# One of eight later modulation vectors computed on TensorE beside layer 1's input projection instead of on VectorE beside layer 0's FFN

## The chip, the cores and the metric

The kernel runs on one core of one Trainium2 chip. The metric is device time in microseconds (us), the median of several executions.

## The reference

Two layers of a backbone are applied to 128 context tokens and 128 latent tokens of width 2048. Both streams go through the same weights, each with its own modulation. Cut to what matters, one layer is:

```
m = silu(cond) @ w_mod + b_mod                 # 2048 x 12288, cut in six vectors of 2048
sm, cm, gm, sf, cf, gf = split(m, 6)           # vectors 0 to 5 of the layer
h = rms_norm(x, g_pre) * (1 + cm) + sm
z = h @ w_in                                   # 2048 x 4608
o = attention A, attention B, gated mixing of z
x = x + gm * rms_norm(o @ w_out, g_post)       # 2048 x 2048
h = rms_norm(x, g) * (1 + cf) + sf
x = x + gf * rms_norm((silu(h @ w_gate) * (h @ w_up)) @ w_down, g2)   # inner width 5632
```

`cond` is `c_ctx` for the context and `c` for the latent tokens. With two layers there are twelve modulation vectors. Each needs a 2048 x 2048 block of `mod_w` (16.8 MB in f32) for two rows of output. Vector 8 is layer 1's `gm`, the gate of its mixer: it is first needed when layer 1's attention begins.

## The kernel before

All weights are streamed from HBM once, in pieces of 256 rows by 512 columns (512 KB). A dense product runs in units of eight pieces (one chunk of 512 output columns). For each piece SyncE issues the load into `raw` (a ring of four slots), ScalarE casts it to `whi` (line 1094), VectorE makes the remainder `wlo` (line 1362), and TensorE does 12 matmuls of 512 columns (line 792): two halves of the piece, two token streams, three products (`whi,xt_lo`, `wlo,xt_hi`, `whi,xt_hi`). The rings have four slots (`RING`) and ScalarE and VectorE split four pieces ahead of TensorE (`LEAD`). All pieces have one running number g. Layer 0's FFN is g 104 to 367, layer 1's input projection ("win 1" below) g 368 to 439, layer 1's output projection g 440 to 471, layer 1's FFN g 472 to 735. An FFN is cut in three groups: up and gate units, then the down units of the group. Layer 0's down groups start at g 168, 264 and 344. The last one has four chunks of six pieces (g 344 to 367).

The modulation vectors are computed beside this, in either of two ways.

On TensorE (`MOD_PE`, `mod_quarter`, line 852): a vector is 32 pieces of `mod_w`, put in the ring `mraw` (four slots), as four chunks of eight. A burst of four pieces is 8 matmuls, each recorded as two rows; they put 32 columns of `cond` against 512 columns of weights, and four of them go to four separate partition groups of bank M. After the last chunk, ScalarE copies bank M to `mrow` (line 1123), TensorE turns it (`vector_turn`, line 872) and VectorE copies bank T to `modt` (line 1403). Before, vectors 2 (beside layer 0's input projection), 3 and 4 (attention and output projection of layer 0), 9 and 10 (the same of layer 1) go this way; layer 1's input projection carries none.

On VectorE (`MOD_DVE`): at certain g, right behind the split of piece g, `accumulate` multiplies one 128 x 1024 piece of `mod_w` by one element of `cond` per partition and adds it to `acc`, once for each of the two conditions (line 1384, or 1381 for the first of a sum). When the 32 pieces of a vector are in, TensorE sums over the partitions (line 782, `MOD_REDUCE`, behind its piece g), ScalarE copies the row behind its cast of piece g + 3 (`MOD_ROW`), TensorE turns it behind piece g + 2 (`MOD_TAIL`), VectorE copies it behind its split of g + 9 (`MOD_COLS`). Before, vectors 5, 6, 7 and 8 go this way in layer 0's FFN, 128 pieces spread evenly over g 111 to 363, and vector 11 in layer 1's FFN.

Work of an engine runs in the order of the program. On VectorE, where an up group ends, the order is: the splits of the unit (which reach four pieces into the down group), `multiply` (line 1750, makes `hid`), later `ht_lo` (line 1757). TensorE, behind the first piece of the down group, waits for `hid` to transpose it (line 880). In the last down group VectorE also adds each chunk to `f` (line 1793) and multiplies by the gate (line 1587); ScalarE squares `f` between (line 1108).

SyncE issues all weight loads in one order. A `raw` load waits until the slot's piece was split (`lo_ready`), a `mod_w` load waits in `mod_room` until the piece four earlier in the ring `mraw` was used; whatever is behind it in the program waits with it.

Between two stages lies a turnover: `rms_norm` of the finished rows, the new x, its transposes. Its last part overlaps the first four pieces of the next stage, which TensorE takes for one token stream, then for the other (`APART`).

Of the kernel before, what the change touches and what calls it, by code (L numbers as in the profile page):

```python
# [17 lines left out]
CH = 512  # L18
# [5 lines left out]
W_INC = W_IN // CH  # L24
# [13 lines left out]
UNIT = KD // KB  # L38
RING = 4
LEAD = 4  # L40
# [3 lines left out]
IN_FIRST, IN_SECOND = {3: range(0, 4)}, {3: range(4, 8)}  # L44
LOAD_ONE = {0: [0], 1: [1], 2: [2], 3: [3], 4: [4], 5: [5], 6: [6], 7: [7]}
LOAD_FIRST, LOAD_SECOND = ({0: [j], 2: [j + 1], 4: [j + 2], 6: [j + 3]} for j in (0, 4))
# [3 lines left out]
MOD_WIN = W_INC // 2  # L50
# [3 lines left out]
APART = 4  # L54
# [17 lines left out]
def edge_of(l, which):  # L72
# [4 lines left out]
OUT_MODS = {3: (0, range(0, 4)), 8: (0, range(4, 8)), 13: (1, range(0, 4)), 19: (1, range(4, 8)), 24: (2, range(0, 4))}  # L77
OUT_FETCH = {4: (0, (0, 1)), 5: (0, (2, 3)), 11: (0, (4, 5)), 12: (0, (6, 7)), 16: (1, (0, 1)), 17: (1, (2, 3)),
             22: (1, (4, 5)), 23: (1, (6, 7)), 27: (2, (0, 1)), 28: (2, (2, 3)), 31: (2, (4, 5, 6, 7))}
MOD_PE = [2, 3, 4, 9, 10]  # L80
MOD_DVE = [5, 6, 7, 8, 11]
MPIECES = 2 * KD
FFN_PIECE = [104, 472]
DVE_SPAN = 252


def dve_piece_at(v, i):

    if v == 11:
        return FFN_PIECE[1] + 8 + 5 * i // 2  # L90
    return FFN_PIECE[0] + 7 + DVE_SPAN * (MPIECES * MOD_DVE.index(v) + i) // (4 * MPIECES - 1)


def dve_reduce_at(v):

    return dve_piece_at(v, MPIECES - 1)
# [3 lines left out]
MOD_FETCH = {g - 3: e for g, e in DVE_PIECES.items()}  # L100
MOD_REDUCE = {dve_reduce_at(v): v for v in MOD_DVE}
MOD_TAIL = {dve_reduce_at(v) + 2: v for v in MOD_DVE}
MOD_ROW = {dve_reduce_at(v) + 3: v for v in MOD_DVE}
MOD_COLS = {dve_reduce_at(v) + 9: v for v in MOD_DVE}


def dve_op(v, i, s=0):
# [80 lines left out]
class Plan:  # L188
# [3 lines left out]
    def __init__(self):  # L192
        self.unit, self.mod, self.use = 0, 0, dict.fromkeys(BANKS, 0)

        self.fills, self.fill = dict.fromkeys(BANKS, 0), {}
        self.at = {}
        self.turn_bank = 0
        self.acc_bank = 0

        self.mark(("init",))  # L200
        self.take("X0")
        self.mods(MOD_INIT)
        for l in range(DEPTH):
            self.pre(l, 0)
            self.mark((l, "win"))
            self.unit += W_INC
            self.mods(0 if l else MOD_WIN)
            self.takes(["A0", "A1"], (W_INC + 1) // 2 if l else ND * W_INC // 2)
            self.takes(["B0", "B1"], W_INC // 2 if l else ND * W_INC // 2)
            self.mark((l, "att"))  # L210
            self.attention(l)
            self.mark((l, "out"))
            self.unit += ND
            self.takes(["A0", "A1", "B0", "B1"], ND // 2)
            self.mods(MOD_OUT + 1)
            self.pre(l, 1)
            for g, (_, n) in enumerate(GROUPS):
                self.mark((l, "up", g))
                self.unit += 2 * n
                self.takes(["A0", "A1", "B0", "B1", "X0", "X1"], n)  # L220
                if g == 1:
                    self.gate(l, 1)
                self.mark((l, "down", g))
                self.unit += n if n < 4 else ND
                self.takes(["A0", "A1", "B0", "B1"], ND // 2)
# [56 lines left out]
def build_program(nc, a):  # L282
    plan = Plan()
# [7 lines left out]
    with ExitStack() as ctx:  # L291
# [192 lines left out]
        def _(sp):  # L484
# [44 lines left out]
            def both(u, w, col, m=0, l=0, behind={}, js=range(UNIT)):  # L529

                for j in js:
                    piece(u, j, w[j * KB * P:(j + 1) * KB * P, bass.ds(col, CH)])
                    if j in behind:
                        mod_chunk(m, l, behind[j])
# [29 lines left out]
                    mod_chunk(m, 0, js)  # L564
            for l in range(DEPTH):
                if l:
                    u, _, _ = plan.at[(l, "win")]
                    w = a["w_in"][l]
                    both(u, w, 0, js=range(LEAD, UNIT))
                    for i in range(1, W_INC):  # L570
                        both(i + u, w, i * CH)
                u, m, _ = plan.at[(l, "out")]
                w = a["w_out"][l]
                first_unit(u, w, 0)
                for step, _, m_att in plan.at[(l, "attention")]:
                    if step[0] == "mod_first":
                        mod_chunk(m_att, l)
                for q in range(LEAD, ND * UNIT):
                    i, j = divmod(q, UNIT)
                    both(u + i, w, i * CH, js=[j])  # L580
                    if q in OUT_FETCH:
                        mi, js = OUT_FETCH[q]
                        mod_chunk(m + mi, l, js)
                first_unit(plan.at[(l, "up", 0)][0], a["w_gate"][l], 0)
                for g, (c0, n) in enumerate(GROUPS):
                    u, _, _ = plan.at[(l, "up", g)]
                    both(u, a["w_gate"][l], c0 * CH, js=range(0 if g else LEAD, UNIT))
                    for i in range(0, n - 1):
                        chunk(i * 2 + (u + 1), a["w_up"][l], 0, i * CH + c0 * CH)
                        chunk(i * 2 + (u + 2), a["w_gate"][l], 0, i * CH + (c0 + 1) * CH)  # L590
                    chunk(u + 2 * n - 1, a["w_up"][l], 0, (c0 + n - 1) * CH)
                    u, m, _ = plan.at[(l, "down", g)]
                    if n == 4:
                        for i in range(0, ND):
                            chunk(i + u, a["w_down"][l], c0 * CH, i * CH)
                    else:
                        for i in range(ND):
                            chunk(u, a["w_down"][l], c0 * CH, i * CH, 2 * n, 2 * n * i)
                if l + 1 < DEPTH:
                    first_unit(plan.at[(l + 1, "win")][0], a["w_in"][l + 1], 0)  # L600
# [137 lines left out]
        def _(pe):  # L738
# [8 lines left out]
            def dense(u, pair, i, hi, lo, nk=KD, ph=0, ready=None, m=None, behind={}, first=0, last=0):  # L747

                free(pair + "0", i)
                free(pair + "1", i)
                n = nk // KB
                for js in (range(first), range(first, n - last), range(n - last, n)):
                    together = js.start == first and js.stop == n - last
                    for streams in [(0, 1)] if together else [(0,), (1,)]:
                        for j in js:
                            if streams[0] == 0:
                                pe.wait_ge(lo_ready, u * UNIT + (ph + j + 1))
                            slot = (ph + j) % RING  # L760
                            for kb in range(KB):
                                k = j * KB + kb
                                if ready:
                                    ready(k, streams)
                                mm = products(pair, k, hi, lo, slot, kb, nk, streams=streams)
                            if streams[-1] == 0:
                                if j == n - 1:
                                    mm.then_inc(half_done, 1)
                                continue
                            mm.then_inc(w_used, 1)  # L770
                            if j in behind:
                                mod(m, behind[j])
                            dve_vector(u * UNIT + ph + j)
# [222 lines left out]
            pe.wait_ge(cond_ready, 1)  # L996
            start()
            for l in range(DEPTH):
                u, _, use = plan.at[(l, "win")]

                def pair(i, ready=None):
                    dense(i * 2 + u, "A", i + use["A0"], xt_hi, xt_lo, ready=ready, first=APART if ready else 0)
                    dense(i * 2 + (u + 1), "B", i + use["B0"], xt_hi, xt_lo)

                if l:
                    pair(0, pre(l, 0))
# [59 lines left out]
        def ahead(split, u, ph=0, pieces=UNIT, between=None, leave=0, late=None):  # L1066


            for j in range(pieces - leave):
                split(u, ph + LEAD + j)  # L1070
                if late:
                    late(j)
                if between and j == pieces - 1 - max(leave, 1):
                    between()
# [8 lines left out]
        def _(act):  # L1083
# [190 lines left out]
                    square(x[:, s, n * CH:(n + 1) * CH], ssx[:, s, n:n + 1])  # L1274
            start()
            for l in range(DEPTH):
                u, _, _ = plan.at[(l, "win")]
                if l:
                    ahead(split, u, late=lambda j: pre_late(l, 0, j))
                    for i in range(1, W_INC):  # L1280
                        ahead(split, i + u)
                attention(l)
                u, m, use = plan.at[(l, "out")]
                for i in range(ND):
# [60 lines left out]
        def _(dve):  # L1345
# [363 lines left out]
            normal(0, 0, 0, 1, 2, 3)  # L1709
            start()  # L1710
            for l in range(DEPTH):
                u, _, use = plan.at[(l, "win")]

                def pair(i):
                    ahead(split, i * 2 + u, late=None if i else lambda j: pre_late(l, 0, j))
                    read_out(i * 2 + u, i * 2 * CH, "A")
                    ahead(split, i * 2 + (u + 1))
                    read_out(i * 2 + (u + 1), i * 2 * CH + CH, "B")

                if l:  # L1720
                    for i in range(W_INC // 2):
# [119 lines left out]
```

## Time and profile before

| | us |
|---|---|
| median of 3 runs | 2442.37 |
| lowest, highest | 2436.07, 2445.17 |
| the profiled execution, its own time | 2445.17 |
| its span (first to last instruction) | 2443.4 |
| TensorE busy / VectorE busy / ScalarE busy | 2310.0 / 1578.3 / 984.4 |

The profile is one execution. Its span is 1.8 us less than its time. Shares of busy time are averages over stages; what an edit is worth is read in the stage where it acts. The three runs lie 9.1 us apart.

### The profile page before, as it was taken

The numbers are of one execution on the slowest core, as the hardware profiler recorded it, in microseconds if no ns is written. First come the engines' busy times: TensorE is split into PE (matmuls) and PEld (weight loads), VectorE is DVE, ScalarE is ACT, GpSimd is POOL, SyncE is SP. The second block draws the span as 40 slices with busy tenths as digits, with TensorE's granted clock in tenths as the row PEclk, the third lists the DMA queues.
The fourth block names the chain that finished last, engine by engine and source line by source line (L and its number), as shares of the span: only waits on it lengthen the run. The fifth ranks groups of instructions, "written<-read, shape, count | busy, mean of one in ns | idle before, by whom it ended". The sixth has DMA issues, their size and how long they took to land.

```text
span 2443.4 us, 28114 instructions
## 1 busy us (share of the span) xinstructions
PE 2310.0 (95%) x10780; PEld 1806.2 (74%) x10780; DVE 1578.3 (65%) x1715; ACT 984.4 (40%) x1253; POOL 67.5 (3%) x97
## 2 busy tenths in 40 slices
PE   4999878989999999999998998798999999999998
PEld 1776645768878888788776885576888888878886
DVE  2555444479988889889886454446888644554455
ACT  2333232454444444334345344335444444434443
POOL 1000020000000000000000102000000000000000
PEclk8999988999999999999999999999999999999999
DMA  8779978858878878788864766885877666656664
GB/s 302 254 281 340 332 274 288 303 193 303 284 254 299 288 265 293 246 280 289 298 198 155 215 208 233 286 300 197 278 268 252 220 196 189 189 182 192 191 221 147
DMA packets 269319, 609.93 MB, mean 250 GB/s; under 512 B 19117, under 2 KB 19297, under 8 KB 267841
## 3 DMA queue, kind: packets, MB, share of 16 engines
q1 hardware_dynamic: 264832, 589.37, 71.5%
q0 software_dynamic: 4352, 18.76, 2.2%
q8 instruction: 86, 1.41, 0.2%
q14 instruction: 49, 0.39, 0.0%
HBM read 603.79 MB, written 5.45 MB: 249 GB/s over the span
## 4 chain that ended last, share of the span: by engine, by line
PE 84%; DMA 6%; DVE 4%; issue 2%; ACT 2%; SPq 0%; POOL 0%; DVEq 0%; POOLq 0%; ACTq 0%
PE bank_A L792 39%; PE bank_B L792 38%; DMA mraw<-in_mod_w 6%; PE bank_M L852 3%; PE bank_X L880 2%; DVE wlo L1362 1%; PE bank_M L841 1%; ACT whi L1094 1%; PE bank_T L872 1%; DVE xtmp L1443 1%; DVE x L1475 0%; DMA raw<-in_w_out 0%; DVE acc L1384 0%; PE bank_M L782 0%; ACT xtmp L1137 0%
## 5 line engine op out<-in xcount | busy, mean ns | idle before, releaser
L1362 DVE TENSOR_TENSOR wlo<-raw,whi 128x1024 fp32r<-128x1024 f32 x736 | 896.7, 1223 | 687.2 <-ACT whi L1094 687.0
L1094 ACT CAST whi<-raw 128x1024 fp32r<-128x1024 f32 x736 | 770.3, 1050 | 1190.8 <-PE bank_A L792 591.3
L792 PE MATMUL bank_A<-whi,xt_lo 128*128 128x512 f32 x1136 | 452.1, 398 | 17.9 <-DVE xt_lo L1413 11.1
L792 PE MATMUL bank_A<-wlo,xt_hi 128*128 128x512 f32 x1136 | 446.8, 393 | 0.0
L792 PE MATMUL bank_A<-whi,xt_hi 128*128 128x512 f32 x1136 | 446.5, 393 | 0.0
L792 PE MATMUL bank_B<-whi,xt_lo 128*128 128x512 f32 x1104 | 433.4, 393 | 0.5 <-issue 0.5
L792 PE MATMUL bank_B<-wlo,xt_hi 128*128 128x512 f32 x1104 | 430.0, 389 | 0.0
L792 PE MATMUL bank_B<-whi,xt_hi 128*128 128x512 f32 x1104 | 429.7, 389 | 0.0
L1384 DVE SCALAR_TENSOR_TENSOR acc<-mraw,cond,acc 128x1024 f32<-128x1024 f32 x300 | 371.2, 1279 | 0.0
L792 PEld LDWEIGHTS bank_A<-whi,xt_lo 128*128 128x128 f32 x1136 | 215.9, 190 | 84.5 <-issue 28.1
L792 PEld LDWEIGHTS bank_A<-whi,xt_hi 128*128 128x128 f32 x1136 | 215.8, 190 | 46.0
L792 PEld LDWEIGHTS bank_B<-whi,xt_lo 128*128 128x128 f32 x1104 | 207.3, 188 | 56.2 <-issue 13.4
L792 PEld LDWEIGHTS bank_A<-wlo,xt_hi 128*128 128x128 f32 x1136 | 215.9, 190 | 43.5
L792 PEld LDWEIGHTS bank_B<-whi,xt_hi 128*128 128x128 f32 x1104 | 207.2, 188 | 43.6
L792 PEld LDWEIGHTS bank_B<-wlo,xt_hi 128*128 128x128 f32 x1104 | 207.3, 188 | 42.0
L792 PE MATMUL bank_A<-whi,ht_lo 128*128 128x512 f32 x352 | 139.2, 395 | 0.7 <-DVE wlo L1362 0.7
L792 PE MATMUL bank_A<-wlo,ht_hi 128*128 128x512 f32 x352 | 138.3, 393 | 0.0
L792 PE MATMUL bank_A<-whi,ht_hi 128*128 128x512 f32 x352 | 137.9, 392 | 0.0
L792 PE MATMUL bank_B<-whi,ht_lo 128*128 128x512 f32 x352 | 137.5, 391 | 0.2 <-DVE wlo L1362 0.2
L792 PE MATMUL bank_B<-wlo,ht_hi 128*128 128x512 f32 x352 | 137.0, 389 | 0.0
L792 PE MATMUL bank_B<-whi,ht_hi 128*128 128x512 f32 x352 | 137.0, 389 | 0.0
L852 PE MATMUL bank_M<-mraw,cond 128*32 128x512 f32 x640 | 93.4, 689 | 30.7 <-DMA mraw<-in_mod_w 30.7
(193 smaller groups left out, 1432.9 us busy)
## 6 DMA issues: line engine op xcount, KB each, us to landing
mraw<-in_mod_w SPq DMA_DIRECT2D x384, 512.0 KB, 6.0
raw<-in_w_gate SPq DMA_DIRECT2D x176, 512.0 KB, 4.4
raw<-in_w_up SPq DMA_DIRECT2D x176, 512.0 KB, 4.4
raw<-in_w_down SPq DMA_DIRECT2D x176, 512.0 KB, 4.8
raw<-in_w_in SPq DMA_DIRECT2D x144, 512.0 KB, 4.7
raw<-in_w_out SPq DMA_DIRECT2D x64, 512.0 KB, 5.8
gate_mix<-gate_rows POOLq DMA_DIRECT2D x4, 1024.0 KB, 6.6
gate_ffn<-gate_rows POOLq DMA_DIRECT2D x4, 1024.0 KB, 9.0
```

Of the source, the lines that this page charges most:

```text
L792: mm = pe.matmul(bank[f"{pair}{s}"][:], xs[:, k, t], ws_[:, slot, kb, :], start=(k == first and n == 0), stop=(k == (nk - 1 if last is Non ...
L841: mm = pe.matmul(bank["M"][g:g + 32, :], cond[:, 2 * k:2 * k + 32], mraw[:, j % RING, kb, :], start=(k < 4), stop=(k >= KD - 4))
L852: mm = pe.matmul(bank["M"][32 * c:32 * c + 32, :], cond[:, 2 * k:2 * k + 32], mraw[:, ring_piece(m, j + c // 2) % RING, c % 2, :], start=( ...
L872: mm = pe.matmul(bank["T"][:, w * t:w * t + w], mrow[:, t * P:(t + 1) * P], sel[:], start=True, stop=True)
L880: mm = pe.transpose(bank[b][:, n * P:(n + 1) * P], t, ident[:])
L1094: act.copy(whi[:, ph % RING], raw[:, ph % RING]).then_inc(hi_ready, 1)
L1362: dve.tensor_tensor(wlo[:, ph % RING], raw[:, ph % RING], whi[:, ph % RING].bitcast(F32), ALU.subtract).then_inc(lo_ready, 1)
L1384: ins = dve.scalar_tensor_tensor(out=acc[:, h, s, :], in0=w, scalar=c, in1=acc[:, h, s, :], op0=ALU.mult, op1=ALU.add)
L1443: ins = dve.tensor_scalar(xtmp[:, b % 2, s, t, :], bank[bk][:, t * P:(t + 1) * P], scal[:, k, s:s + 1], shift[:, k, s:s + 1], ALU.mult, AL ...
```

## The change

Vector 8 moves from `MOD_DVE` to `MOD_PE`. The planner gives layer 1's input projection four chunks of modulation, like layer 0's: a burst of four pieces behind the fourth piece of each of its first eight units, the row and turn behind the eighth unit. The loads of these 32 pieces are put between the `raw` loads of those units (`LOAD_FIRST`, `LOAD_SECOND`: behind the loads of pieces 0, 2, 4, 6 of a unit; the first two ahead of the unit's fifth piece). `IN_FIRST`, `IN_SECOND`, `LOAD_FIRST` and `LOAD_SECOND` were in the file already. Vectors 5, 6 and 7 keep VectorE and are now placed at g = 112, 196, 280 plus 5i/2 rounded down, for i from 0 to 31 (so five splits carry two pieces). Each ends 77 pieces after its start, at g 189, 273 and 357. The row copy on ScalarE moves from g + 3 to g + 5 behind the reduction, the column copy on VectorE from g + 9 to g + 8; this holds for vector 11 too.

```
-MOD_PE = [2, 3, 4, 9, 10]
-MOD_DVE = [5, 6, 7, 8, 11]
+MOD_PE = [2, 3, 4, 8, 9, 10]
+MOD_DVE = [5, 6, 7, 11]
-DVE_SPAN = 252
+DVE_FIRST = {5: FFN_PIECE[0] + 8, 6: FFN_PIECE[0] + 92, 7: FFN_PIECE[0] + 176, 11: FFN_PIECE[1] + 8}
 def dve_piece_at(v, i):
-    if v == 11:
-        return FFN_PIECE[1] + 8 + 5 * i // 2
-    return FFN_PIECE[0] + 7 + DVE_SPAN * (MPIECES * MOD_DVE.index(v) + i) // (4 * MPIECES - 1)
+    return DVE_FIRST[v] + 5 * i // 2
-MOD_ROW = {dve_reduce_at(v) + 3: v for v in MOD_DVE}
-MOD_COLS = {dve_reduce_at(v) + 9: v for v in MOD_DVE}
+MOD_ROW = {dve_reduce_at(v) + 5: v for v in MOD_DVE}
+MOD_COLS = {dve_reduce_at(v) + 8: v for v in MOD_DVE}
...
-            self.mods(0 if l else MOD_WIN)
+            self.mods(MOD_WIN)
...
-                    u, _, _ = plan.at[(l, "win")]
+                    u, m, _ = plan.at[(l, "win")]
                     w = a["w_in"][l]
-                    both(u, w, 0, js=range(LEAD, UNIT))
-                    for i in range(1, W_INC):
-                        both(i + u, w, i * CH)
+                    both_rest(u, w, 0, m, l)
+                    both(u + 1, w, CH, m, l, LOAD_SECOND)
+                    for i in range(1, W_INC // 2):
+                        both(i * 2 + u, w, i * 2 * CH, i + m, l, LOAD_FIRST)
+                        both(i * 2 + (u + 1), w, i * 2 * CH + CH, i + m, l, LOAD_SECOND)
+                    both(u + W_INC - 1, w, (W_INC - 1) * CH)
...
-                    dense(i * 2 + u, "A", i + use["A0"], xt_hi, xt_lo, ready=ready, first=APART if ready else 0)
-                    dense(i * 2 + (u + 1), "B", i + use["B0"], xt_hi, xt_lo)
+                    dense(i * 2 + u, "A", i + use["A0"], xt_hi, xt_lo, ready=ready, m=i + m, behind=IN_FIRST,
+                          first=APART if ready else 0)
+                    dense(i * 2 + (u + 1), "B", i + use["B0"], xt_hi, xt_lo, m=i + m, behind=IN_SECOND)
+                    mod_tail(i + m)
...
-                    for i in range(1, W_INC):
-                        ahead(split, i + u)
+                    ahead(split, u + 1, between=lambda: mod_row(m))
+                    for i in range(1, W_INC // 2):
+                        ahead(split, i * 2 + u)
+                        ahead(split, i * 2 + (u + 1), between=lambda: mod_row(i + m))
+                    ahead(split, u + W_INC - 1)
...
                     read_out(i * 2 + (u + 1), i * 2 * CH + CH, "B")
+                    mod_cols(i + m)
```

## Rows read from the trace of the kernel before

**Rows 1.** The page: busy time of the engines, and the chain that ended last

```profile
PE 2310.0 (95%) x10780; PEld 1806.2 (74%) x10780; DVE 1578.3 (65%) x1715; ACT 984.4 (40%) x1253; POOL 67.5 (3%) x97
PE 84%; DMA 6%; DVE 4%; issue 2%; ACT 2%; SPq 0%; POOL 0%; DVEq 0%; POOLq 0%; ACTq 0%
```

**Rows 2.** Busy us by stretch (PE, PEld, DVE, ACT, POOL), PE clock, DMA share, GB/s

```profile
549.25:1206.65 657.40, 651.93 (x2940) 535.47 (x2939) 576.28 (x523) 271.57 (x286) 0.55 (x1) 1.00 0.82 280
1206.65:1282.10 75.45, 71.78 (x320) 56.60 (x319) 61.42 (x67) 31.97 (x46) 1.64 (x3) 0.98 0.68 233
1282.10:1315.40 33.30, 24.48 (x104) 18.80 (x104) 26.73 (x53) 21.10 (x44) 2.02 (x3) 0.85 0.31 95
1315.40:1500.00 184.60, 182.85 (x816) 149.85 (x816) 96.19 (x89) 70.95 (x69) 9.22 (x13) 1.00 0.70 216
1720.00:2366.60 646.60, 644.33 (x2891) 532.08 (x2890) 385.56 (x347) 269.76 (x284) 0.55 (x1) 1.00 0.67 214
```

**Rows 3.** Chain of work: start us, us; a unit in layer 0's FFN, one in win 1

```profile
571.01 21.77 PE bank_A L792 x96
...
1342.90 21.76 PE bank_A L792 x96
```

**Rows 4.** Timeline of TensorE, a burst in layer 1's output projection: start us, us

```profile
1593.29 1.92 PE L852 MATMUL bank_M<-mraw,cond 128*32 128x512 f32 x16
1595.14 0.50 PE L792 MATMUL bank_A<-whi,xt_lo 128*128 128x512 f32 x1
```

**Rows 5.** Timeline of TensorE: vector 8's reduction and turn, with the matmul behind each

```profile
1267.56 1.92 PE L782 MATMUL bank_M<-acc,ones_row 128*32 128x512 f32 x16
...
1269.41 0.50 PE L792 MATMUL bank_B<-whi,ht_lo 128*128 128x512 f32 x1
...
1278.28 0.95 PE L872 MATMUL bank_T<-rsel,mrow 128*128 128x8 f32 x8
1279.09 0.48 PE L792 MATMUL bank_B<-whi,ht_lo 128*128 128x512 f32 x1
```

**Rows 6.** Timeline of VectorE and TensorE at the starts of four down groups

```profile
706.62 0.39 PE L792 MATMUL bank_A<-whi,ht_hi 128*128 128x512 f32 x1
708.20 0.99 PE L880 MATMUL bank_X<-ident,hid 128*128 128x128 f32 x6 [1.19 <-DVE wlo L1362]
...
978.99 2.48 DVE L1384 SCALAR_TENSOR_TENSOR acc<-mraw,cond,acc 128x1024 f32<-128x1024 f32 x2
...
979.00 0.39 PE L792 MATMUL bank_A<-whi,ht_hi 128*128 128x512 f32 x1
982.16 1.21 PE L880 MATMUL bank_X<-ident,hid 128*128 128x128 f32 x8 [2.78 <-issue]
...
1213.54 0.63 PE L792 MATMUL bank_A<-wlo,ht_hi 128*128 128x512 f32 x1
1213.97 0.63 PE L792 MATMUL bank_A<-whi,ht_hi 128*128 128x512 f32 x1
...
1877.32 0.39 PE L792 MATMUL bank_A<-whi,ht_hi 128*128 128x512 f32 x1
1878.08 1.10 PE L880 MATMUL bank_X<-ident,hid 128*128 128x128 f32 x7 [0.38 <-issue]
```

**Rows 7.** Timeline of TensorE from layer 0's last down group into the turnover

```profile
1256.45 0.50 PE L792 MATMUL bank_A<-whi,ht_lo 128*128 128x512 f32 x1 [0.67 <-DVE wlo L1362]
...
1272.65 0.50 PE L792 MATMUL bank_B<-whi,ht_lo 128*128 128x512 f32 x1 [0.19 <-DVE wlo L1362]
1285.76 1.97 PE L880 MATMUL bank_X<-ident,f 128*128 128x128 f32 x8 [3.70 <-DVE f L1429]
```

**Rows 8.** Raw loads of win 1, then of 1388 to 1392, issue to landing

```profile
DMA to landing us min/median/max: 4.2/4.5/11.8
...
DMA to landing us min/median/max: 8.9/10.3/11.8
```

**Rows 9.** Timeline of ScalarE in win 1 while GpSimd's attention loads run

```profile
1403.40 1.05 ACT L1094 CAST whi<-raw 128x1024 fp32r<-128x1024 f32 x1 [4.60 <-DMA raw<-in_w_in]
```

More of the change, by code:

```diff
@@ L998, in _ @@
             for l in range(DEPTH):
-                u, _, use = plan.at[(l, "win")]
+                u, m, use = plan.at[(l, "win")]
                 def pair(i, ready=None):
-                    dense(i * 2 + u, "A", i + use["A0"], xt_hi, xt_lo, ready=ready, first=APART if ready else 0)
-                    dense(i * 2 + (u + 1), "B", i + use["B0"], xt_hi, xt_lo)
+                    dense(i * 2 + u, "A", i + use["A0"], xt_hi, xt_lo, ready=ready, m=i + m, behind=IN_FIRST,
+                          first=APART if ready else 0)
+                    dense(i * 2 + (u + 1), "B", i + use["B0"], xt_hi, xt_lo, m=i + m, behind=IN_SECOND)
+                    mod_tail(i + m)
                 if l:
@@ L1276, in _ @@
             for l in range(DEPTH):
-                u, _, _ = plan.at[(l, "win")]
+                u, m, _ = plan.at[(l, "win")]
                 if l:
                     ahead(split, u, late=lambda j: pre_late(l, 0, j))
-                    for i in range(1, W_INC):
-                        ahead(split, i + u)
+                    ahead(split, u + 1, between=lambda: mod_row(m))
[3 more added lines that the diff above has]
+                    ahead(split, u + W_INC - 1)
                 attention(l)
@@ L1711, in _ @@
             for l in range(DEPTH):
-                u, _, use = plan.at[(l, "win")]
+                u, m, use = plan.at[(l, "win")]
                 def pair(i):
```

## The prediction

> **What bounds the kernel now.** I read the page first: TensorE is busy 95% of the span, and 84% of the chain that ended last is TensorE's own work, against 4% of VectorE [rows 1]. So I looked at where TensorE is not the bound. The busy time by stretch compares the two FFNs, which do the same dense work [rows 2]. Layer 0's runs with VectorE busy 576.28 of 657.40 us (88%), layer 1's with 385.56 of 646.60 (60%), and TensorE is busy over 99% in both. The chain shows a unit of 96 matmuls at 21.77 us in layer 0's FFN and 21.76 in win 1 [rows 3], that is 0.227 us a matmul and 2.72 a piece. A saturated VectorE beside it does not slow a unit. What VectorE costs layer 0's FFN must lie in gaps between units. I went through TensorE's timeline for these, from the start of one matmul to the start of the next, in both FFNs.
>
> **What the change adds.** Vector 8 needs 32 pieces, in eight bursts. In the timeline of layer 1's output projection a burst starts at 1593.29 and the next dense matmul at 1595.14 [rows 4]: 1.85 us in which TensorE does nothing else. The ten full bursts of the two output projections that stand between dense matmuls all read so. Win 1 is 182.85 us busy of 184.60 [rows 2], so no idle time takes them in. Eight bursts: 8 x 1.85 = +14.8. The first comes in the turnover, behind piece g 371, ahead of the last transpose of x; the casts and subtractions that follow that transpose end just when TensorE wants piece 374, so it counts in full too. The turn of the row, 0.81 (1278.28 to 1279.09, [rows 5]), is now paid behind the eighth unit: +0.8. ScalarE's row copy stands one piece (2.72) ahead of it, more than its cast and copy take; the copy of bank T on VectorE is covered by the unit after. Together +15.6 in win 1.
>
> **What it removes on TensorE.** Vector 8's reduction, from 1267.56 to the matmul at 1269.41, is 1.85, and its turn 0.81 [rows 5]: -2.7. So TensorE's own work grows by 12.9.
>
> **What VectorE's relief gives.** 32 pieces of two accumulations (2.48 us a pair, [rows 6]) leave VectorE in layer 0's FFN, some 79 us. Most of that is idle time handed to an engine that was not the bound. It counts only at the gaps I found:
>
> 1. Where a down group starts, TensorE waits after one piece for `hid`. Without an accumulation near it the gap is 0.76 (1877.32 to 1878.08, layer 1, [rows 6]). An accumulation behind the last split ahead of `multiply` stands in front of it: 979.00 to 982.16, 3.16, with the pair on VectorE at 978.99 [rows 6]. One behind the split before that, as at 706.62 to 708.20, makes it 1.58 [rows 6]. The old formula for the places gives pieces at g 168 and 170, at 265 and 267, and at 345 and 347; the last split ahead of `multiply` is g 171, 267, 347. The traced gaps fit that. The new places are 169; 266; 345 and 347. So the first group goes from 1.58 to 0.76 (-0.8), the second from 3.16 to 1.58 (-1.6), the third stays at 3.16.
> 2. Behind the long gaps matmuls run at 0.43 a step (1213.54 to 1213.97, [rows 6]) instead of 0.227 for a few us: seven or eight of them, 1.5 us. That goes in the second group with its gap (-1.5) and stays in the third.
> 3. In the last down group old pieces stand every other g up to 363, ten of them; of the new ones six, the last at 357. TensorE waits for `wlo` at 1256.45 (0.67) and 1272.65 (0.19) [rows 7], with the slower steps around them 1.1 in all; layer 1's group, with no accumulations, has next to none. With two pieces instead of three in the second chunk, and none behind it, I reckon VectorE ready some 2 us before it is wanted: -1.1.
>
> Sum: -0.8 - 1.6 - 1.5 - 1.1 = -5.0. The later row copy costs nothing: at g + 5 ScalarE waits for g + 1, and cast and copy end inside piece g + 2. Vector 7's reduction and turn now lie in the third chunk of the last down group, ahead of the turnover, at their old price. The turnover itself loses the row copy on ScalarE and the small copy on VectorE, off the chain I followed; I count nothing, and keep as a bound TensorE's wait of 3.70 at its start [rows 7].
>
> **The queue of SyncE.** Each `mod_w` load of a unit waits for the burst of the unit before. Behind it stands `raw` piece 1 of the next unit, which would have gone out when piece 5 was split, about 3.8 us earlier. I worked out its slack in TensorE pieces: issued just after the burst of a unit begins, it is wanted 15.4 us after that begins, less 2.3 for cast and subtraction; it lands in 4.5 us, the median of win 1 [rows 8]. That leaves about 8, so no stall. Traffic in win 1 goes from 216 GB/s [rows 2] to 284 (216 over 184.6 us is 39.9 MB; with 16.8 MB more in 200 us), which layer 0's FFN holds (280, [rows 2]) with no stall.
>
> **Total.** +15.6 - 2.7 - 5.0 = +7.9 us, say +8. Against the profiled execution's own 2445.17 that is 2453; that execution was the slowest of three, 2.8 above the median, so for the median of the new kernel I take 2442.4 + 8 = 2450.4.
>
> Bounds: if none of the three gains comes, +12.9; if all that sets layer 0's FFN apart from layer 1's goes (the third long gap with its slow steps, 4.0 more), +4. The best end adds the turnover's wait of 3.70: +0.
>
> **Rivals.**
>
> *SyncE's order starves TensorE in win 1 (slower).* For it: one queue carries both rings, and a blocked `mod_w` load holds the `raw` loads. The weak place is where GpSimd's attention loads run: `raw` landings rise to a median of 10.3 and at most 11.8 us [rows 8], and a ScalarE cast starts after 4.60 us of waiting [rows 9]; TensorE did not wait. Its slack there is about 14.3 us from issue to landing. If extra traffic and the 3.8 us of blocking add 5 us to the worst landing, TensorE loses 2 to 3 us once: +11. If it happens at every unit, at 3 us each, +8 + 8 x 3 = +32, or 2474. It decides from the point where landings pass 12 to 13 us regularly. Against it: layer 0's FFN runs one `mod_w` load to two `raw` loads all through, the same mix, and the blocking thins traffic just then.
> The Trainium skill (DMA: Bandwidth & Descriptors, Queues, rings and completion order) says that a DMA engine with work in several queue rows alternates between them. By that rule SyncE's queue has half of the engines while GpSimd's loads run; over 12 us (the longest landing) at half of 280 GB/s that is 3.2 pieces, where 4.4 `raw` pieces and half as many of `mod_w` are wanted: 3.4 pieces short, or 6.4 us at full rate, against about 10 of slack (14.3 less the median landing). The trace's late cast agrees with the rule for the old traffic; for the new it would put the case at the edge, which is why I give the rival more than a token chance.
>
> *VectorE's relief gives nothing (slower by 13).* The gaps are set by ScalarE or loads, not by accumulations. Against it: the three groups' gaps follow the places of the accumulations exactly. 2455.3.
>
> *The turnover gains (faster).* With no accumulation in its last two chunks, the turnover behind layer 0's FFN could lose its idle time and its low clock: 33.30 us at a clock of 0.85, 24.48 busy [rows 2]. Even all of the 8.8 idle us leaves -1, no measurable gain; faster by over 0.5% would also need bursts that hide, and [rows 4] speaks against that.
>
> **How the numbers follow.** About 0.5% (12 us) is what a measurement of this kernel can tell from no change. My sum stands at +0.3%. Its own range is +4 to +13, with 4 us of scatter between medians (three runs spread over 9.1 us). Chances: the sum 0.72 (0.60 within 0.5%, 0.10 slower, 0.02 faster through scatter); starving 0.13 (0.11 slower); no relief 0.10 (0.06 slower); turnover gain 0.05 (0.02 faster). That makes faster 0.04, same 0.69, slower 0.27. The range: low 2441 (the best bound less a little scatter), high 2463 (no relief, a few us of starving, scatter).
>
> **What would show it.** Rows of line 852 in win 1, x16 and eight of them, each 1.85 to the next dense matmul; the stage 15 to 16 us longer with TensorE still 99% busy; no TensorE wait on `raw` or `wlo` in it. The gaps at the starts of layer 0's down groups: 0.76, 1.58, 3.16. VectorE busy some 79 us less in layer 0's FFN and the stretch from its start to the turnover 7 to 8 us shorter. It would be wrong if TensorE waits for `wlo` or for `mraw` in win 1, if bursts there cost other than 1.85, if new waits arise at vector 7's reduction in the last down group, or if the turnover changes by more than 2 us.

## The result, and the profile after

| | before | after |
|---|---|---|
| median of 11 runs each, us | 2445.17 | 2457.20 |
| lowest to highest | 2436.07 to 2449.35 | 2446.18 to 2463.11 |
| ratio of after to before | | 1.0053, 95% interval 1.0038 to 1.0068 |
| profiled execution, its own time | 2445.17 | 2467.93 |
| its span | 2443.4 | 2466.1 |

The change makes the kernel slower by 0.53%, 13 us by the ratio (9 to 17) and 12.0 by the medians. I had said +8, with +4 to +13 for the likeliest case alone. My 2450.4 stood on the median of three runs, 2442.37; with eleven runs the kernel before is at 2445.17, so 2.8 of the 6.8 us between 2450.4 and 2457.20 lie in the base and 4.0 in the sum. The profiled execution of after happens to be slower than all eleven timed ones, 10.7 us over their median; its stages are therefore read beside a second profile of each kernel below.

The page of the changed kernel, its busy times by engine (share of the span, instructions):

```profile
PE 2332.2 (95%) x10892; PEld 1816.3 (74%) x10892; DVE 1507.0 (61%) x1651; ACT 984.2 (40%) x1253; POOL 67.5 (3%) x97
```

VectorE is 71.3 us less busy than in [rows 1], where I had said some 79, and TensorE 22.2 more. The same stretches as in [rows 2], by their landmarks in the new trace (columns as there):

```profile
549.72:1203.14 653.42, 650.34 (x2916) 535.33 (x2915) 516.02 (x466) 270.61 (x285) 0.55 (x1) 0.99 0.79 260
1203.14:1277.06 73.92, 71.01 (x320) 56.80 (x319) 51.88 (x60) 31.42 (x44) 1.64 (x3) 0.98 0.69 225
1277.06:1314.61 37.55, 27.61 (x121) 20.50 (x122) 27.83 (x53) 22.41 (x47) 1.84 (x3) 0.82 0.42 127
1314.61:1514.70 200.09, 198.41 (x937) 152.79 (x935) 95.61 (x90) 71.08 (x69) 9.24 (x13) 1.00 0.79 270
1741.30:2389.30 648.00, 645.74 (x2891) 532.90 (x2890) 384.94 (x347) 269.70 (x284) 0.55 (x1) 1.00 0.69 213
```

Layer 0's FFN body is 4.0 us shorter with 60 us less on VectorE. Win 1 (fourth row) is 15.5 longer; TensorE fills 99% of it, and DMA moves 270 GB/s instead of 216. The trace has no wait of TensorE in win 1, and SyncE waits there for a burst six times, at most 6.4 us, at no cost to anyone.

A burst in win 1, in TensorE's timeline (start us, us):

```profile
1330.34 0.39 PE L793 MATMUL bank_B<-wlo,xt_hi 128*128 128x512 f32 x1
1330.57 0.39 PE L793 MATMUL bank_B<-whi,xt_hi 128*128 128x512 f32 x1
1330.89 1.92 PE L853 MATMUL bank_M<-mraw,cond 128*32 128x512 f32 x16
1332.74 0.50 PE L793 MATMUL bank_B<-whi,xt_lo 128*128 128x512 f32 x1
1333.08 0.40 PE L793 MATMUL bank_B<-wlo,xt_hi 128*128 128x512 f32 x1
```

From the burst to the next dense matmul it is 1.85 us, as in [rows 4]. But look at its neighbours: the step (from one start to the next) into the burst is 0.32 and the step behind it 0.34, where dense matmuls step by 0.227. The edges of a burst cost about 0.2 us more, which I had left out.

Then the starts of the three down groups of layer 0's FFN, to be read against [rows 6]:

```profile
707.25 0.39 PE L793 MATMUL bank_A<-whi,ht_hi 128*128 128x512 f32 x1
708.02 0.63 PE L881 MATMUL bank_X<-ident,hid 128*128 128x128 f32 x4 [0.38 <-issue]
...
975.72 0.39 PE L793 MATMUL bank_A<-whi,ht_hi 128*128 128x512 f32 x1
977.29 0.88 PE L881 MATMUL bank_X<-ident,hid 128*128 128x128 f32 x5 [1.19 <-DVE wlo L1368]
...
1205.47 0.39 PE L793 MATMUL bank_A<-whi,ht_hi 128*128 128x512 f32 x1
1208.63 1.94 PE L881 MATMUL bank_X<-ident,hid 128*128 128x128 f32 x8 [2.77 <-issue]
```

The gaps are 0.77, 1.57 and 3.16 us, where I had said 0.76, 1.58 and 3.16. Not as I had said: the matmuls behind the second group's start still run slow in this profile.

```profile
980.01 0.61 PE L909 MATMUL bank_X<-ident,gatev 128*32 128x128 f32 x2 [1.51 <-DVE ht_lo L1764]
980.55 0.79 PE L793 MATMUL bank_A<-whi,ht_lo 128*128 128x512 f32 x1
981.14 0.63 PE L793 MATMUL bank_A<-wlo,ht_hi 128*128 128x512 f32 x1
981.56 0.63 PE L793 MATMUL bank_A<-whi,ht_hi 128*128 128x512 f32 x1
```

The step is 0.42 (981.14 to 981.56) instead of 0.227; the granted clock from 981.0 to 984.5 is 0.50, that is the level of 1.2 instead of 2.4 GHz. So a gap of 3.16 us is not needed for slow steps. A second wait, of 1.51 us for `ht_lo` (1.49 in one profile), stands behind the gap in every version, and eleven slow steps follow it here. In the second profile of the same kernel, below, none follows it, and eight stand behind the third group's gap, where the first profile has one. Which of the two places runs slow is scatter in these profiles; what decides it is not shown. The wait at the turnover behind this FFN grew as well, from 3.70 [rows 7] to 4.45:

```profile
1276.66 0.39 PE L793 MATMUL bank_B<-whi,ht_hi 128*128 128x512 f32 x1
1281.50 0.90 PE L881 MATMUL bank_X<-ident,f 128*128 128x128 f32 x3 [4.45 <-DVE f L1435]
```

The turn of vector 8's row used to lie between the two token streams of the last chunk. VectorE's chain from the first stream's addition to `f` (1275.76 in before, 1271.65 in after) to this transpose takes 10.0 and 9.85 us in the two, so TensorE had time for the turn. Without it, most of its 0.81 us comes back here as waiting.

### The profile page after: what moved, and what is told of

It reads as the page before. It is cut to its first block, busy times and chain, and to the rows that moved or that the text cites. A ratio compares the mean times of both kernels' runs of the same rounds, so it can differ in the third digit from the quotient of the medians.

```text
span 2466.1 us, 28259 instructions
## 1 busy us (share of the span) xinstructions
PE 2332.2 (95%) x10892; PEld 1816.3 (74%) x10892; DVE 1507.0 (61%) x1651; ACT 984.2 (40%) x1253; POOL 67.5 (3%) x97
## 4 chain that ended last, share of the span: by engine, by line
PE 87%; DMA 5%; DVE 4%; ACT 2%; issue 1%; POOL 0%; SPq 0%; DVEq 0%; POOLq 0%; ACTq 0%
PE bank_A L793 40%; PE bank_B L793 38%; DMA mraw<-in_mod_w 5%; PE bank_M L853 3%; PE bank_X L881 2%; PE bank_M L842 1%; DVE wlo L1368 1%; DVE x L1481 0%; PE bank_T L873 0%; ACT whi L1097 0%; DVE xtmp L1449 0%; PE bank_M L783 0%; PE bank_B L970 0%; ACT junk L1111 0%; PE bank_A L970 0%
## 5 line engine op out<-in xcount | busy, mean ns | idle before, releaser
L1390 DVE SCALAR_TENSOR_TENSOR acc<-mraw,cond,acc 128x1024 f32<-128x1024 f32 x240 | 297.1, 1280 | 0.0
L793 PEld LDWEIGHTS bank_B<-whi,xt_lo 128*128 128x128 f32 x1104 | 207.2, 188 | 59.7 <-issue 16.8
L853 PE MATMUL bank_M<-mraw,cond 128*32 128x512 f32 x768 | 106.4, 662 | 32.1 <-DMA mraw<-in_mod_w 32.0
```

The source lines that it names most:

```text
L793: mm = pe.matmul(bank[f"{pair}{s}"][:], xs[:, k, t], ws_[:, slot, kb, :], start=(k == first and n == 0), stop=(k == (nk - 1 if last is Non ...
L853: mm = pe.matmul(bank["M"][32 * c:32 * c + 32, :], cond[:, 2 * k:2 * k + 32], mraw[:, ring_piece(m, j + c // 2) % RING, c % 2, :], start=( ...
L1390: ins = dve.scalar_tensor_tensor(out=acc[:, h, s, :], in0=w, scalar=c, in1=acc[:, h, s, :], op0=ALU.mult, op1=ALU.add)
```

## The experiments

Stretches below are read from TensorE's timeline in each profile: layer 0's FFN from the last transpose of x ahead of it (537.4 in before) to the first behind it (1285.8 in [rows 7]); the turnover from there to its last transpose of x (1309.3); win 1 from there to its last dense matmul (1494.8). "Slow" counts single dense steps of 0.36 to 0.45 us in layer 0's FFN.

The last column is the sum of the three stages against the mean of the two profiles of before.

| kernel | ratio to before (95%) | layer 0's FFN | slow | turnover | win 1 | sum |
|---|---|---|---|---|---|---|
| before | 1 | 748.4 | 14 | 23.5 | 185.6 | -0.4 |
| before, again | one time | 749.1 | 14 | 23.5 | 185.6 | +0.4 |
| after | 1.0053 (1.0038 to 1.0068) | 743.5 | 13 | 27.0 | 201.0 | +13.7 |
| after, again | one time | 741.1 | 9 | 25.4 | 201.0 | +9.7 |
| thin bursts | 0.9985 (0.9965 to 1.0004) | 741.1 | 7 | 23.8 | 189.6 | -3.3 |
| no vector 8 | 0.9956 (0.9942 to 0.9971) | 743.6 | 14 | 25.0 | 185.5 | -3.6 |
| after, free splits | 1.0023 (1.0006 to 1.0041) | 736.4 | 2 | 27.0 | 201.0 | +6.6 |
| after, all three hit | 1.0071 (1.0050 to 1.0092) | 750.3 | 23 | 27.0 | 201.0 | +20.5 |
| after, old row places | 1.0052 (1.0032 to 1.0071) | 741.0 | 8 | 25.4 | 201.0 | +9.7 |
| vector 8 on VectorE in win 1 | 0.9953 (0.9937 to 0.9970) | 737.9 | 7 | 23.3 | 187.7 | -8.9 |
| the same, after's places | 0.9969 (0.9956 to 0.9983) | 743.6 | 14 | 25.1 | 187.7 | -1.5 |
| before, three pieces moved by one | 0.9954 (0.9936 to 0.9972) | 741.8 | 6 | 23.6 | 185.6 | -6.9 |

**The kernel before again, and after again.** No edit.

> The kernel before once more, for a second profile. The two profiles so far differ by 7.0 us in the stretch from layer 1's attention to the end of its turnover, where the change edits nothing. If that is scatter of the waits on mod_w loads in the attention (one theory), this profile lies between or beyond the two (204 to 213 us from the last dense matmul of win 1 to the last transpose of x, known so far as 212.6 and 219.6). If the change causes it (the other), this profile repeats 212.6 within 1 us.

> The changed kernel once more. Scatter: its stretch from layer 1's attention to the last transpose of x is nearer to 212.6 than to 219.6 us. Caused by the change: 219 to 220 again. In both cases the ledger of the earlier stages repeats: layer 0's FFN 4 to 5 us shorter than before, win 1 15 us longer, and the turnover between them 3.5 us longer (1.85 of it the first burst).

Single times 2451.36 and 2453.67. The stretch in question, by its summed stages, is 220.0 us in the second profile of before (213.2 in the first; the expectation's figures start one row later) and 220.0 in the second of after: it is scatter. My expectation for after's second profile was wrong (it lay at the upper value, not the lower), but before reaches that value by itself. The scatter is not in the waits for `mod_w` loads, where I had looked for it. From the last dense matmul of win 1 to the first transpose of x, in the first and the second profile of before (columns as in [rows 2]):

```profile
1494.83:1684.33 189.50, 162.57 (x917) 110.85 (x915) 90.61 (x134) 75.31 (x143) 16.20 (x18) 0.95 0.78 275
```

```profile
1494.36:1689.08 194.72, 167.42 (x916) 113.58 (x915) 90.72 (x134) 75.28 (x143) 16.17 (x18) 0.92 0.77 267
```

TensorE waits 12.5 us for `mod_w` loads in the one and 12.0 in the other. What differs is its busy time, 4.9 us more for as many matmuls, at a granted clock of 0.92 instead of 0.95. The rest is the turnover behind, which takes 23.7 to 23.9 or 25.3 us, whatever the kernel. Over all twelve profiles this stretch takes 210.1 to 220.1 us (first part at a clock of 0.98 to 0.91), and the stretch ahead of layer 0's FFN, where no edit changes the work but for one `memset`, 529.1 to 538.0. The time of one profiled execution therefore says little about a few us. The sum of the three stages leaves this scatter out.

In the second profile of after the FFN is 7.6 us shorter than the mean of before's two and the turnover 1.9 longer, where I had expected 4 to 5 and 3.5; win 1 is 15.5 longer, and the sum is +9.7. The first profile gives -5.3, +3.5 and +15.5, +13.7 in all. Their mean is +11.7.

Its chain over win 1 shows the burst's full price (start us, us):

```profile
1307.25 10.88 PE bank_B L793 x48
1318.13 1.85 PE bank_M L853 x16
1319.98 11.15 PE bank_B L793 x48
1331.13 10.88 PE bank_A L793 x48
1342.01 1.85 PE bank_M L853 x16
1343.86 11.15 PE bank_A L793 x48
```

48 dense matmuls take 10.88 us ahead of a burst and 11.15 behind it: a burst costs 1.85 + 0.27 = 2.12. A unit with one is 23.88 us (1318.13 to 1342.01), one without 21.76 [rows 3]. The trace of before has the same price in layer 1's output projection, behind the burst of [rows 4], by its chain of work:

```profile
1593.36 1.85 PE bank_M L852 x16
1595.21 11.15 PE bank_A L792 x48
```

**Thin bursts.** Vector 8's matmuls stream 32 of their 512 columns. What is left out: 15 of 16 parts of vector 8. Loads and waits all stay.

```
             def mod_quarter(m, js):
+                n = 32 if vector_of(m) == 8 else CH
...
-                        mm = pe.matmul(bank["M"][32 * c:32 * c + 32, :], cond[:, 2 * k:2 * k + 32],
-                                       mraw[:, ring_piece(m, j + c // 2) % RING, c % 2, :], ...)
+                        mm = pe.matmul(bank["M"][32 * c:32 * c + 32, 0:n], cond[:, 2 * k:2 * k + 32],
+                                       mraw[:, ring_piece(m, j + c // 2) % RING, c % 2, 0:n], ...)
```

> The changed kernel, but vector 8's matmuls in win 1 stream 32 of the 512 weight columns (the rest of vector 8 is left out); all loads and waits stay. If TensorE's time in the bursts is what win 1 costs, a burst falls from 1.85 to 0.5 to 0.9 us and the kernel is 8 to 11 us faster than the changed one, about +2 to +4 over before. If the loads or SyncE's blocked order cost it, it stays at the changed kernel's +12.

Measured 0.9985: 16.6 us less than after by the two ratios, whose intervals are each some 4 us wide to either side; by the profile 11.4 in win 1 and 1.6 to 3.2 in the turnover. It is below the range I gave (2 to 4 us over before): layer 0's FFN is 7.6 us shorter in this profile, where the first profile of after had shown 4.9, and a thin burst is shorter than I thought:

```profile
1322.64 0.39 PE L793 MATMUL bank_B<-whi,xt_hi 128*128 128x512 f32 x1
1322.96 0.33 PE L855 MATMUL bank_M<-mraw,cond 128*32 128x32 f32 x16
1323.22 0.50 PE L793 MATMUL bank_B<-whi,xt_lo 128*128 128x512 f32 x1
1323.56 0.39 PE L793 MATMUL bank_B<-wlo,xt_hi 128*128 128x512 f32 x1
```

0.26 us a burst, with the same edges (0.32 into it, 0.34 behind it). All 16.8 MB are still loaded in the same order and TensorE waits for none of them: win 1 is 4.0 us longer than before, which is seven of these bursts with their edges (7 x 0.48 = 3.4) and the turn of 0.8. SyncE still waits for bursts here, up to 5.8 us, and the stage is within 0.2 us of what bursts and turn add up to. So loads and blocking cost nothing in win 1; the columns streamed on TensorE do.

**No vector 8.** Vectors 5 to 7 as in after; vector 8 is neither loaded nor computed, its columns are set to zero.

```
-MOD_DVE = [5, 6, 7, 8, 11]
+MOD_DVE = [5, 6, 7, 11]
+MOD_ALL = [2, 3, 4, 5, 6, 7, 9, 10, 11]
...
+            dve.memset(modt[:, 8 * KD * 2:9 * KD * 2], 0.0)
```

> Vectors 5, 6, 7 placed as in the changed kernel, vector 8 not computed anywhere and its 16.8 MB not loaded (its result is left out, set to zero). Against before this is VectorE's relief alone: by the prediction -5.0 -2.7 = -7.7 us; by the changed kernel's profile, where layer 0's FFN was only 4.9 shorter, -3 to -5. If relief gives nothing, -2.7. Against the thin-burst kernel it shows what loads and leftover bursts cost: 4 to 8 us if only the leftover bursts and the turn do, over 10 if the loads do.

`MOD_ALL` is the order in the ring and of the turns.

Measured 0.9956, 10.8 us less than before (7 to 14), more than either of my figures. The stages show 5.1 less in the FFN, 1.5 more in the turnover and nothing in win 1, -3.6 in all. In this kernel's and after's profiles the FFN is 5 to 8 us shorter; about 2 of that is vector 8's reduction, which TensorE no longer makes there, and 3 to 5.5 are relief. Had relief given nothing, -2.7 would have been measured, and the interval excludes that. What lies above the stages in the 10.8 I can assign to none; the profiled execution was the slowest of nine (2446.98 against a median of 2437.64). Between this kernel and the thin bursts lie 7.1 us by the two ratios, within my 4 to 8 for leftover bursts and the turn alone.

**Free splits.** One line of after; no accumulation behind g 170, 171, 266, 267, 346 or 347.

```
-DVE_FIRST = {5: FFN_PIECE[0] + 8, 6: FFN_PIECE[0] + 92, 7: FFN_PIECE[0] + 176, 11: FFN_PIECE[1] + 8}
+DVE_FIRST = {5: FFN_PIECE[0] + 8, 6: FFN_PIECE[0] + 89, 7: FFN_PIECE[0] + 174, 11: FFN_PIECE[1] + 8}
```

> The changed kernel with vector 6 placed from g 193 and vector 7 from g 278, so that no accumulation stands behind the last two splits ahead of a multiply (g 170, 171, 266, 267, 346, 347 all free). If accumulations there make the gaps at the starts of down groups, all three gaps are 0.76 to 0.77 us, the slow matmuls behind the third vanish, and the kernel is 3 to 5 us faster than the changed one (+8 to +9 over before). If the gaps come from ScalarE or loads, nothing changes (+12).

**All three hit.** The same line with 7, 93 and 176.

```
+DVE_FIRST = {5: FFN_PIECE[0] + 7, 6: FFN_PIECE[0] + 93, 7: FFN_PIECE[0] + 176, 11: FFN_PIECE[1] + 8}
```

> The changed kernel with vector 5 from g 111 and vector 6 from g 197, so that g 171, 267 and 347 all carry an accumulation. By the placement theory all three gaps are 3.16 us: 2.4 + 1.6 more than the changed kernel in gaps and 1 to 3 in slow matmuls behind them, so +17 to +19 over before. By the rival, no change (+12).

These two do the same work on every engine and ran on one chip: 2451.63 (+5.6 over before by its ratio) and 2460.66 (+17.4). The first is some 2 us below my range, the second in it. The two medians lie 9.0 us apart, the two ratios 11.7. The third group's start with free splits, then the second's with all three hit:

```profile
1196.21 0.39 PE L793 MATMUL bank_A<-whi,ht_hi 128*128 128x512 f32 x1
1196.98 0.63 PE L881 MATMUL bank_X<-ident,hid 128*128 128x128 f32 x4 [0.38 <-issue]
```

```profile
975.50 0.39 PE L793 MATMUL bank_A<-whi,ht_hi 128*128 128x512 f32 x1
978.66 1.10 PE L881 MATMUL bank_X<-ident,hid 128*128 128x128 f32 x7 [2.77 <-issue]
```

All three gaps are 0.76 to 0.77 in the one and 3.16 in the other. Three gaps of 2.4 explain 7.2 of the 13.9 us between their FFNs; most of the rest is 21 more slow steps at 0.2 (4.2 us) and transposes that run slow too (0.6 each, twice). Where three accumulations stand is worth more than whether vector 8's 32 pairs are there: with all splits free, the FFN is 741.8 us with them (the last kernel below) and 736.4 without them, and about 2 of those 5.4 are vector 8's reduction.

**Old row places.** `MOD_ROW` back at + 3, `MOD_COLS` at + 9.

> The changed kernel with the row copy back at g + 3 and the column copy at g + 9. My prediction counted this part at nothing: within 1 us of the changed kernel (+12). If the stall that it takes from ScalarE mattered, it is 1 to 2 us slower for each of four vectors, +16 or more.

1.0052 against after's 1.0053. The interval is some 5 us wide to either side, but all three stages repeat the second profile of after within 0.1 us: this part of the change shows no effect, as I had counted.

**Vector 8 on VectorE in win 1.** From before, with the free splits and, for the other vectors, after's row places. TensorE gets nothing new; `acc` lies under `z` in that stage, so vector 8 is summed in `qkt`, `ckt` and `turned_b`, which the attention fills later.

```
+DVE_FIRST = {5: 112, 6: 193, 7: 278, 8: 376, 11: 480}
 def dve_piece_at(v, i):
+    return DVE_FIRST[v] + (2 * i if v == 8 else 5 * i // 2)
...
+        def acc_at(v, h, s):
+            if v != 8:
+                return acc[:, h, s, :]
+            t = qkt[:, 8 * s:8 * s + 8, :] if h == 0 else (ckt if s == 0 else turned_b)[:, 0:8, :]
+            return t.rearrange("p a b -> p (a b)")
```

> Vector 8 stays on VectorE, but in win 1 (every other piece from g 376 to 438, summed in buffers that the attention fills later), with vectors 5 to 7 placed as in the kernel with free splits. Nothing is added to TensorE. If VectorE's relief in layer 0's FFN is worth what I think and win 1 takes the accumulations beside full TensorE work, as layer 0's FFN did at the same density, it is faster than before by 5 to 9 us. If VectorE, about 95% busy in win 1 then, makes TensorE wait there, or the loads do, it is 0 to 10 us slower than before.

0.9953: 11.5 us faster than before, more than I expected, and 24 faster than after. Win 1 from 1300 to 1477 us in this kernel, then the same 177 us of before (columns as in [rows 2]):

```profile
1300.00:1477.00 177.00, 176.97 (x781) 146.24 (x780) 162.11 (x148) 69.74 (x67) 8.16 (x12) 1.00 0.88 296
```

```profile
1315.00:1492.00 177.00, 176.95 (x781) 146.29 (x780) 91.61 (x84) 69.06 (x67) 8.17 (x12) 1.00 0.69 212
```

VectorE goes from 52% to 92% busy and DMA from 212 to 296 GB/s, and TensorE makes the same 781 matmuls. Here is the pair of facts of this case: win 1 has room on VectorE and on the DMA engines, and none on TensorE. (The table's 187.7 for it against 185.6 holds vector 8's reduction, 1.85 and its edges, which layer 0's FFN no longer pays.) Not all of the 11.5 comes from moving vector 8: the last kernel below has the free splits alone.

**The same with after's places** for vectors 6 and 7 (196, 280).

> The kernel with vector 8 on VectorE in win 1, but vectors 6 and 7 at the changed kernel's places (g 196 and 280), so that gaps of 1.57 and 3.16 us stay in layer 0's FFN. By the placement theory it gives back the 4 to 5 us between the two changed placements: 6 to 8 us faster than before, where the version with free splits measured 11.5. If the places don't matter it is 11 us faster too.

0.9969, 7.6 us faster: by its ratio 4 less than with free splits, as the placement theory has it (4 to 5), and its FFN is 5.7 longer. The two intervals overlap, so the ratios alone would not carry this; the stages do. Against before, however, the stages give 1.5 us and the ratio 7.6 (4 to 11). In the four kernels without bursts in win 1 (this one, the one above it, the one below and no vector 8) the ratio shows 3 to 7 us more than the stages, and the cause stays open.

**Three pieces moved by one.** From before; everything else as before, vector 8 in layer 0's FFN.

```
-    return FFN_PIECE[0] + 7 + DVE_SPAN * (MPIECES * MOD_DVE.index(v) + i) // (4 * MPIECES - 1)
+    g = FFN_PIECE[0] + 7 + DVE_SPAN * (MPIECES * MOD_DVE.index(v) + i) // (4 * MPIECES - 1)
+    return {170: 169, 267: 268, 347: 348}.get(g, g)
```

> The kernel before with three of its 128 accumulations moved by one piece (g 170 to 169, 267 to 268, 347 to 348); vector 8 stays on VectorE in layer 0's FFN. If the places of single accumulations and not VectorE's load as such make layer 0's FFN longer, the three gaps fall to 0.77 us: -0.8 -2.4 -2.4 and 1.5 to 3 of slow matmuls, 6 to 9 us faster than before. If the load matters, the gaps go elsewhere in the group and the gain is under 3 us.

0.9954: 11.3 us faster than before (7 to 16), more than the 6 to 9 I expected, with VectorE as loaded as ever (651.9 us busy in the FFN, 652.0 in before). All three gaps are 0.77 to 0.80 in its trace, and its FFN is 7.0 shorter, which is the surer figure. By the ratios, moving vector 8 to win 1 as well (11.5) adds nothing that can be told from scatter; by the stages, 2 us (8.9 against 6.9). One thing moved instead of vanishing, the wait in the last down group:

```profile
1241.92 0.39 PE L793 MATMUL bank_A<-whi,ht_hi 128*128 128x512 f32 x1
1243.44 0.50 PE L793 MATMUL bank_A<-whi,ht_lo 128*128 128x512 f32 x1 [1.14 <-DVE wlo L1363]
```

1.14 us where [rows 7] had 0.67. Ten accumulations stand between the 24 pieces of that group, beside the additions to `f`, and without vector 8's the waits are gone: there VectorE's load as such seems to count.

## Why the prediction was right, and where its terms were off

**The mechanism was right, and the direction; the size was 8 where 12 to 13 was measured.** Two signs that I had named against myself came up, both in size: a burst costs other than 1.85, and the turnover changed by 1.9 in one profile and 3.5 in the other. By the prediction's own terms:

- *Eight bursts at 1.85, TensorE has no room in win 1: +14.8.* Right in kind; mis-sized. A burst costs 2.12 with its edges: 8 x 2.12 = 17.0, 2.2 more. The rows for it were in the trace of before (11.15 us behind the burst, above); I had measured to the next matmul's start and not on to where the step is regular again. Win 1's +15.5 is seven bursts (7 x 2.12 = 14.8) and the turn (+0.8, right).
- *The first burst counts in full.* Right: in the second profile of after the turnover is 1.9 longer. In three of the five profiles with full bursts in win 1 it is 27.0 and not 25.4; the 1.6 more are slow steps, which turnovers without a burst have at times as well (25.0 and 25.1 against 23.5). What brings them is not shown.
- *Vector 8's reduction and turn leave: -2.7.* Mis-sized: the reduction's 1.85 and its edges do leave (2.1, as win 1 grew with it on VectorE there), but the turn had been hidden behind VectorE's chain in the last chunk; the wait at the turnover grew from 3.70 to 4.45, so about 2.1 was gained. I counted its place in the program and not what waited at the end of the chunk.
- *Gaps at the down groups: -0.8 and -1.6, the third unchanged.* Right to 0.01 us in the trace. Placing all three at will (free, and all hit) set the three gaps to 0.77 and to 3.16 and moved the kernel by 9 us by the medians, 12 by the ratios.
- *Slow steps leave the second group: -1.5.* This failed in size: 13 and 9 slow steps remain in the FFN of after's two profiles, 14 in before's. In the first profile they only changed places, eleven behind the second group and one behind the third; in the second they left the second group and stayed in the third, as I had said. It was worth 0.2 to 1 us.
- *The last down group's waits: -1.1.* Near; they are gone but for one long step of 0.52 in place of 0.227, which leaves 0.9.
- *SyncE's order costs nothing; the row places cost nothing.* The first is shown by the thin bursts (loads complete, 4 us longer, all accounted for); for the second, the old row places show no difference in any stage.

The relief terms and the reduction with its turn made -7.7 in the prediction; the profiles show -5.3 and -7.6. The other side made +15.6; turnover and win 1 show +18.9 and +17.3. The sum of the stages is +13.7 and +9.7 against the measured +9 to +17, so no further term is needed. That the measured time is above my sum comes from the bursts' edges (2.2, less 0.25 for those of the reduction), the hidden turn (0.8) and slow steps; how many slow steps there are differs between profiles of one kernel.

**The rivals.** Starvation in win 1 did not occur: `raw` landings of up to 10.2 us there (10.5 in the second profile) made no wait on TensorE, and the stage moved 270 GB/s where I had worked out 284. The version with vector 8 on VectorE moved 296 GB/s in that stage, with landings of up to 12.4 us, without a wait either. The Trainium skill (DMA: Bandwidth & Descriptors, Queues, rings and completion order) says that a DMA engine alternates between the queue rows that have work. By that rule I had put the case at the edge; no run here shows how the engines were shared, or how near it was. "No relief" was refuted by the kernel with no vector 8, and its reason by the free splits and the three moved pieces: there the places of accumulations alone set the gaps. "The turnover gains" was refuted: it got longer in both profiles of the changed kernel, and with neither vector 8 nor a burst it was 25.0 against 23.5.

## What to carry to other kernels

Before work is moved off an engine, ask which single instructions of it stand ahead of something the bound engine waits for; here three of 128 accumulations, each moved by one place, gave 11 us (7 of them seen in the stage), and the move of thirty-two to the bound engine cost 12. Work belongs in a stage where its own engine has room and the bound engine is untouched: the same vector put on VectorE in the same stage, with the better places, gave 11.5 us where the better places alone gave 11.3; its cost there can't be told from scatter, where the bursts cost 17. And the price of a foreign burst between dense matmuls is to be measured unit to unit, not from its start to its end.

## What the runs showed that I had not expected

- The edges of a 32-column burst among 128-column matmuls cost 0.22 to 0.27 us for each burst, the same for bursts of 1.85 and of 0.26 us.
- A gap of 1.57 us and, behind it, a wait of 1.51 were followed by eleven steps of 0.42 us in one profile of after and by none in the other. With all gaps at 0.77 and the wait of 1.51 still there, five slow steps followed it in before with three pieces moved, and none in after with free splits.
- Two profiles of one unchanged kernel differ by 6.8 us in one stretch of 213 and 220 us: 4.9 of it is TensorE busy longer at a lower granted clock (0.92 against 0.95) with the same waits for loads, 1.6 is the turnover. One profile decides nothing about 5 us unless the stages that the edit does not touch are compared too.
